# A fused Mamba-2, attention and hybrid block on one NeuronCore: the products of ones by ones in TensorE's waits are left out

## The reference

```python
# first block
hn = rms_norm(x, g_pre[0])
h  = x + mamba2_mixer(hn, ...)            # projections, conv, scan in chunks of 256, gated norm, output
k_nope, k_rope, v = mla_shared_kv(h, ...)
h  = h + mla_mixer(rms_norm(h, g_pre[1]), ...)   # 16 heads, causal
x  = rms_norm(h, g_final)
# second block
hx = modulate(rms_norm_2(x, norm1), sh1, sc1)
attn_x = gqa_attention(qx, [kx, kc], [vx, vc])   # 8 heads on 2 key heads, 256 context tokens beside
gla_x  = gla_output(ox_f + flip_t(ox_b), go, gla_norm)
x = x + gt1 * ((sigmoid(ga) * (attn_x @ w_br_attn) + sigmoid(gg) * (gla_x @ w_br_gla)) @ w_out)
x = x + gt2 * (square(relu(modulate(rms_norm_2(x, norm2), sh2, sc2) @ w_mlp1)) @ w_mlp2)
```

## Time and profile before

| what | value |
|---|---|
| time, median of 3 runs | 1767.51 us (1764.97, 1767.51, 1768.28) |
| time of the profiled execution | 1765.45 us |
| its span, first to last instruction | 1763.7 us |
| mean granted TensorE clock | 0.997 of 2.4 GHz |
| busy: PE, PEld, DVE, ACT, POOL | 1703.5, 1385.9, 1022.8, 842.7, 707.4 us |

### The profile page before, as it was taken

How to read it: one execution, slowest core, us unless ns; L and a number is a source line. 1 busy time by engine, 2 the same in 40 slices (tenths; PEclk the granted TensorE clock), 3 DMA queues, 4 the chain that set the end, 5 groups by cost and what they waited for, 6 DMA issues and landing times.

```text
span 1763.7 us, 24698 instructions
## 1 busy us (share of the span) xinstructions
PE 1703.5 (97%) x8751; PEld 1385.9 (79%) x8751; DVE 1022.8 (58%) x1600; ACT 842.7 (48%) x1472; POOL 707.4 (40%) x795
## 2 busy tenths in 40 slices
PE   8999999978999999999989999999999999999999
PEld 6877777756777667878878888888888888888887
DVE  5578685677458864466659747766634443232322
ACT  4465665776365664356642354465522332323131
POOL 3634344424442105311114332333245555555554
PEclk9999999999999999999999999999999999999999
DMA  6452633222321002210138621111133323333333
GB/s 209 120 169 85 190 94 117 88 84 60 88 85 53 25 13 76 59 37 25 37 129 258 198 61 37 48 48 49 48 96 96 96 72 97 97 103 97 96 96 108
DMA packets 217150, 160.55 MB, mean 91 GB/s; under 512 B 8333, under 2 KB 190614, under 8 KB 217046
## 3 DMA queue, kind: packets, MB, share of 16 engines
q1 hardware_dynamic: 201758, 125.50, 24.8%
q10 hardware_dynamic: 15288, 33.66, 5.6%
HBM read 156.98 MB, written 2.16 MB: 90 GB/s over the span
## 4 chain that ended last, share of the span: by engine, by line
PE 61%; issue 15%; POOL 9%; DVE 8%; ACT 7%; DMA 1%; POOLq 0%; DVEq 0%; ACTq 0%; SPq 0%
PE ps L658 13%; PE ps L662 13%; PE ps L659 12%; POOL wl L608 9%; PE ps L3123 3%; PE ps L3120 3%; PE ps L3121 3%; PE ps L2187 2%; PE ps L2169 2%; ACT wh L621 1%; PE ps L1644 1%; PE ps L1612 1%; PE ps L2176 1%; PE ps L2684 1%; PE ps L2718 1%
## 5 line engine op out<-in xcount | busy, mean ns | idle before, releaser
L608 POOL TENSOR_TENSOR wl<-raw,wh 128x256 fp32r<-128x256 f32 (+1 forms) x775 | 684.0, 914 | 996.6 <-ACT wh L621 996.6
L658 PE MATMUL ps<-ah,wh 128*128 128x512 f32 (+1 forms) x1144 | 457.8, 400 | 13.1 <-ACT gate_u L2757 4.2
L662 PE MATMUL ps<-ah,wl 128*128 128x512 f32 (+1 forms) x1144 | 447.4, 391 | 0.2
L659 PE MATMUL ps<-al,wh 128*128 128x512 f32 (+1 forms) x1144 | 446.4, 390 | 0.0
L621 ACT ACTIVATE wh<-raw 128x1024 fp32r<-128x1024 f32 (+1 forms) x220 | 230.6, 1049 | 304.7 <-PE ps L662 159.3
L658 PEld LDWEIGHTS ps<-ah,wh 128*128 128x128 f32 (+1 forms) x1144 | 213.9, 187 | 68.0 <-issue 10.2
L662 PEld LDWEIGHTS ps<-ah,wl 128*128 128x128 f32 (+1 forms) x1144 | 213.7, 187 | 49.6 <-POOL wl L608 1.9
L659 PEld LDWEIGHTS ps<-al,wh 128*128 128x128 f32 (+1 forms) x1144 | 214.0, 187 | 44.3 <-issue 1.9
L658 PE MATMUL ps<-bh,wh 128*128 128x512 f32 (+1 forms) x332 | 133.5, 402 | 4.8 <-DVE resid L1469 1.7
L662 PE MATMUL ps<-bh,wl 128*128 128x512 f32 (+1 forms) x332 | 130.6, 393 | 0.8 <-POOL wl L608 0.7
L659 PE MATMUL ps<-bl,wh 128*128 128x512 f32 (+1 forms) x332 | 129.7, 391 | 0.0
(11 more groups left out here) (450 smaller groups left out, 2972.7 us busy)
## 6 DMA issues: line engine op xcount, KB each, us to landing
raw<-w_mlp SPq DMA_DIRECT2D x64, 512.0 KB, 3.9
raw<-w_in SPq DMA_DIRECT2D x52, 512.0 KB, 3.8
raw<-ssm_w_in SPq DMA_DIRECT2D x40, 512.0 KB, 4.0
ada_late<-w_ada ACTq DMA_DIRECT2D x16, 1024.0 KB, 6.1
ada_raw<-w_ada ACTq DMA_DIRECT2D x16, 512.0 KB, 4.4
cum_rows<-cum_saved ACTq DMA_DIRECT2D x16, 512.0 KB, 3.9
raw<-ssm_w_out SPq DMA_DIRECT2D x16, 512.0 KB, 3.4
raw<-mla_w_in SPq DMA_DIRECT2D x11, 512.0 KB, 4.0
```

The lines of the kernel that those rows point to most:

```text
L608: nc.gpsimd.tensor_tensor(wl[:, s, part], raw[:, s, part], wh[:, s, part].bitcast(F32), ALU.subtract).then_inc(lo_ready, LOW_PIECES * (par ...
L658: nc.tensor.matmul(dst, w_hi[k], x_hi[k], start=k == 0, stop=False)
L659: nc.tensor.matmul(dst, w_hi[k], x_lo[k], start=False, stop=False)
L662: ins = nc.tensor.matmul(dst, w_lo[k], x_hi[k], start=False, stop=k == n - 1)
```

## The change

All seven calls of `stay_busy` and the helper itself go. No other instruction is added, removed or put elsewhere; what stood behind the products now stands directly behind what came before them.

```diff
-        def stay_busy(b, n):
-
-            for _ in range(n):
-                nc.tensor.matmul(bank(b)[:, 0:P], ones[:], ones[:], start=True, stop=True)
-
         def pe_start(pe):
             pe.sem_inc(unit_done, CREDIT)
             count_ahead(pe, "pe")
 
             pe.wait_ge(sem("dve_steps"), 2)
-            stay_busy(2, 9)
             pe.wait_ge(sem("ident_in"), 16)
...
             ins_.then_inc(sem("vec_ready"), 1)
-            stay_busy(2, 13)
...
                 output("ssm", g, g, 10, 5, 0)
-                if g == GROUPS - 2:
-                    stay_busy(7, 11)
                 output("ssm", g, g, 10, 5, 1)
...
             output("ssm", GROUPS - 2, GROUPS - 2, 10, 5, 3, lambda: squares(GROUPS - 1))
-            stay_busy(7, 8)
             for w in range(4):
                 output("ssm_last", 0, GROUPS - 1, 0, 0, w)
...
             project_q(0, 1)
-            stay_busy(2, 9)
             scores(0)
...
-                if name == "branch_g" and i == 0:
-                    stay_busy(3, 7)
...
             turn_resid(4)
-            stay_busy(1, 10)
             per_bank = 5
```

## The result

| | before | after |
|---|---|---|
| time, median of 10 runs | 1766.64 us (1763.86 to 1768.28) | 1770.91 us (1770.28 to 1774.61) |
| ratio | | 1.0031, 95% interval 1.0022 to 1.0040 |
| span of the profiled execution | 1763.7 us | 1768.9 us |
| mean granted clock in it | 0.997 | 0.991 |

The kernel is slower by 4.3 us, and the interval excludes that nothing changed. 1771.3 was forecast, in a range of 1766.5 to 1776. The difference that was forecast is 3.8 us, on a base of 1767.51.

The account below looks back on a forecast made before the run. TensorE was taken as the bound, busy for 1703.5 of 1763.7 us. Costs of clock falls, less the small gain, summed to 3.8 us; put on a median of 1767.51 this gave 1771.3 us, range 1766.5 to 1776.

Parts of the forecast that it names:

- Gain of the ones themselves: Third of the seven waits, the only one where the ones outlast the release: removing them gains 0.28 us.
- Price of a fall: A low-clock stretch of 3.4 us loses 1.6 us where TensorE works throughout and sets the pace.
- Place 1: First wait, ahead of the opening transposes: they run slowly, but the sum behind waits for DVE anyway; cost 0.
- Place 2: Second wait, ending at 18.08 us: the fall comes some 3 us sooner; 0.4 us taken.
- Place 4: Fourth wait, ahead of a projection fed by DVE, with 1.4 us of waiting after it; cost 0.1 us.
- Place 5: Fifth wait, by scores, queries and softmax: most of a delay goes on; cost 0.8 us.
- The chances: Chance of a fall behind the bare third to seventh waits: 0.5 third and sixth, 0.7 fourth and fifth, 0.9 seventh.
- Places 6 and 7: Last two waits, dense products behind: 0.8 us, and 1.2 us after 0.3 us of slack.
- Rival B: At the start: transposes don't raise the clock, low until about 24.5 us; 1.2 us more, 1772.5 us; chance 0.07.
- Rival A: Not slower: later waits for DVE or ACT absorb the falls' losses; 1768.5 us; chance 0.33.
- Rival C: Falls come in pairs or last longer behind the third to seventh waits; some 3 us more, 1774.5 us; chance 0.08.
- Rival D: The ones were in the way: 18 us of TensorE time goes, releases come sooner; 1766 us or less; chance 0.02.

Follow-up runs that it names:

- e2_mid: Kernel before without the ones of the third, fourth and fifth waits; 1769.82 us, ratio 1.0020.
- e7_more: Kernel before plus 36 products of ones: 5 in the first projection, 31 ahead of outputs in the last group; 1764.58 us, ratio 0.9987.
- e3_end: Kernel before without the ones of the sixth and seventh waits; 1768.92 us, ratio 1.0014.
- e5_thin: Kernel before with each product of ones cut to 16 columns, same count and weight loads; 1772.43 us, ratio 1.0039.
- e4_turns: Kernel before with transposes in place of the products of ones in the second to seventh waits; 1765.16 us, ratio 0.9998.
- e1_start: Kernel before without the ones of the first two waits; 1767.95 us, ratio 1.0009.

## Why the prediction was right, step by step

- **Gain of the ones themselves.** 0.28 us, at place 3 only. Measured 0.26 in the changed kernel, 0.31 in e2_mid, and zero at places 4 to 7. Right.
- **Price of a fall.** 1.6 us. Measured 1.58 at place 6, 1.57 at place 3 (e2_mid), 1.70 at place 5. Right.
- **Place 1.** The transposes took 6.95 us, all but the last five at the low pace, so they ended at 13.84, 0.1 beyond the worst case of 13.7, and the first sum started at 13.68 instead of 13.47. 0.1 us of it was left at 21 us. Cost nearly 0. Right. The ones there are not sure to raise the clock either: in e7_more, which has them, the transposes kept the low pace until 10.8 us.
- **Place 2.** Put at 0 against this profile, at 1.6 at most against an execution without a fall, and at 0.4 for the median. Measured 0.91 against this profile, which had paid once already, and 2.15 against e3_end, which had not fallen there. The low level lasted 6.8 us instead of 3.4, and the engine was busy for only 2.10 us of the first half. The prediction had said the fall comes sooner, and missed that it then lasts longer. The term was too small, by half or more.
- **Place 4.** 0.1; measured 0, with the clock low from 401.9 to 405.3. The wait for DVE took it all. Right.
- **Place 5.** 0.8, of which a factor of 0.7 for what later stages would take up. They took up nothing: 1.70 when it fell (1.51 in e2_mid, 1.69 in e5_thin). Mis-sized by that factor.
- **The chances.** "Two in three" stood on three waits of one execution, one of which, of 3.26 us, had kept its clock. In ten profiles with that wait bare it kept it twice. Of the ten waits of places 3 to 7 that these experiments and the change left wholly bare, eight were followed by a fall (not place 3 in the changed kernel, not place 4 in e2_mid).
- **Places 6 and 7.** 0.8 and 1.2; the execution paid 1.58 and 1.13. Place 6 had been given a chance of one in two. The clock fell there in both profiled executions that left its wait bare (the changed kernel and e3_end) and in e5_thin, so the chance was likely too low.
- **The number of falls.** Mean clock 0.994 forecast, 0.991 seen. In all runs it went from some 12 us at the low level to 34, so 6 to 7 stretches more instead of 4. The terms were too few and, on average, too dear (0.65 us each in the median, not 1), and the two errors met in the sum. A third error met them: the base was the median of three runs, 1767.51, which lies 0.9 above that of ten (1766.64), while the difference was put 0.5 too low (3.8 for 4.3). That the total came out within half a microsecond is in part luck.
- **Rival B**, transposes that don't raise the clock. In the changed kernel transposes were TensorE's only work before 13.68 us; one by one, they start 0.21 us apart up to 12.8 us and 0.11 apart from 13.35 on, and the sum's two instructions took 1.02 us for both (1.13 before, at the high level). So the clock rose on transposes alone. e4_turns shows that they hold it, too. The Trainium skill says that the high level doesn't engage for transposes ("TensorE: Matmul & The Clock Gate", section "Part 4: PE-mode transpose"); for the float32 transposes of 128 x 128 of this case the measurement decides. The prediction's remark that the ones had just raised the clock before its transposes was not quite so: the first of them still start 0.24 and 0.21 us apart, and the pace doubles at 7.5 us, 1.2 us after the ones end.
- **Rival A**, absorption, was half true: it holds for place 4 and, in the changed kernel, for the stretches from 371 to 396 us (0.77 lost, 0.76 back), and for none of the dense stages.
- **Rival C**, a low level that lasts longer, came true at the start and not behind places 3 to 7. **Rival D**, the ones in the way, holds for place 3 alone, as had been said.

## What to carry to other kernels

Look at the mean granted clock before the slices: 0.997 against 0.991 was the whole effect, and tenths hid it. In this kernel, bound by TensorE, waits of 2 to 3 us that could not be removed were worth filling: products or transposes of 128 columns that end just ahead of the release kept the clock of what follows, 1.1 to 1.7 us a place where that is dense work. Fill that outlasted the wait cost its length (2.46 us for 11 products at place 3), fill of 16 columns gave nothing that the time shows, and ahead of stages that wait again soon (place 4) there was nothing to win. For the price, take what one low stretch loses in dense work, and ask for each place what the next wait will take up. One profile says little on where the clock falls: compare several executions by their mean clock.

## What was not expected of the hardware

- Products of 16 columns with the same weight loads, lasting 2.30 us where those of 128 columns lasted 2.40, did not keep the clock up.
- Transposes both raised it (0.21 us apart up to 12.8 us, 0.11 from 13.35 on, in the changed kernel) and kept it (e4_turns).
- A low stretch can be followed at once by a second one: 6.8 us from 19.7 in the changed kernel, with TensorE busy for 2.10 us of the first 3.4, and 6.8 us from 371.1 in e1_start, with 2.60.
- A wait of 1.23 us at 1118 us was followed by a fall in 4 of 12 profiles, one of 1.73 us at 890 us in none.
- The clock column reads 1.00 before its first record, although the pace shows the low level there: up to 7.5 us in the kernel before and 12.8 in the changed one.
